# Modulation jobs in batches of four, and own places for the first stage's loads

## The chip, the cores and the metric

One Trainium2 chip; the program runs on one of its cores. The metric is device time in microseconds of one execution. A measurement is several executions, of which the median is given.

## The reference, cut to what matters

Two transformer blocks over 256 latent tokens (and 256 context tokens in the first), width 1024, float32. The first block has two layers; each is a mixer (attention beside a convolution of 31 taps) and a PEER stage (top-k choice among 16384 experts). Each stage is modulated: its input is normed, scaled and shifted by vectors that are products of a conditioning vector with a large matrix.

```python
sc, sc_ctx = silu(c), silu(c_ctx)                 # [1024] each
for l in range(2):
    sh1, s1, g1, sh2, s2, g2 = split(sc @ w_mod[l] + b_mod[l], 6)          # w_mod[l]: 1024 x 6144
    csh1, cs1, cg1, csh2, cs2, cg2 = split(sc_ctx @ w_mod[l] + b_mod[l], 6)
    q, k, v, u = split_cols((rms(x) * (1 + s1) + sh1) @ w_in[l])           # w_in[l]: 1024 x 1792
    ...                                           # attention, convolution, output projection
    x = x + g1 * merge_groups(o_attn, o_conv, ...)
    x = x + g2 * peer(rms(x) * (1 + s2) + sh2, ...)
# second block: nine more vectors from c_2
mod = silu(c_2) @ w_ada + b_ada                   # w_ada: 1024 x 9216
```

## The kernel before, in words

Five engine programs (`sync_program`, `tensor_program`, `scalar_program`, `vector_program`, `gpsimd_program`) run side by side; each engine executes its own in order and they meet at counting semaphores. A `Signal` counts what an engine has finished, a `Book` holds which count a label stands for, so `wait_ge(act, ("mrow", k))` waits until ScalarE has done that piece. Tokens lie along the free axis, channels along the 128 partitions.

**Weights.** SyncE streams 1 MB tiles into a ring of `RING` = 4 slots (`load`, L540 to L549). A load waits until the tile four places back in the order has been read, so one blocked load holds all that stand behind it. `columns` loads one tile of 256 weight columns. Where accuracy asks for it a weight tile is split in a high part (ScalarE, `high`, L1313) and a low part (VectorE, `low`, by `tt` at L1893), and PE multiplies high by high, high by low and low by high.

**Modulation jobs.** The matrices w_mod0, w_mod1 and w_ada are cut in 72 tiles of 256 columns; `JOBS` is their order: four scale tiles of layer 0 (`SCALES`), four shift tiles (`SHIFTS`), the rest of layer 0, layer 1, then w_ada. A job has four steps:
- PE, `mod_rows` (L668): eight products of a 32-column stationary slice of `SC` (three columns hold the silu of c, c_ctx and c_2, the others zero) with the weight tile, in four strips of 32 partitions; the trace shows them as 16 instructions;
- ScalarE, `mods` (L1325): the PSUM bank is copied to `mrow`, two copies of which alternate;
- PE, `mod_sum` (L680): two products with the constant `sel` turn the rows into columns and add the four strips;
- VectorE, `mod_bias` (L1893, for scales L1901): the bias is added and the vector written to `MOD` or `ADA`.

PE does the sum of job k in its `mods` call for job k + 1, ahead of that job's rows, or at once where `flush` is set. Jobs are placed by hand beside other work: 8 in the first stage, `SIDE_JOBS` in the steps of each layer's attention (33 in layer 0, 21 in 18 steps of layer 1), and a few around the modulations. All five programs must count them alike.

**PSUM.** `bank` hands out the eight banks in rotation, skips those in `kept`, and waits for the last reader of the bank. During attention banks 0 to 5 are kept, and jobs, taps and the mean share 6 and 7.

**The first stage** (`mixer(0)` in each program). ScalarE issues the DMAs for `vec` (306 KB of small vectors) and `con` (842.5 KB of constants, L1862), SyncE those for xT and the tiles, in the order: six jobs, the first tile of w_in, two jobs, the other tiles of w_in. ScalarE squares x (L1335), PE sums it with the constant `ones` (L700), ScalarE takes the root (L1342), VectorE inverts (L1951), PE spreads it with `pick` (L716). VectorE multiplies x by scale and root, chunk by chunk of 128 channels (L1901), after each pair the next job's bias. Then it makes the low parts of the first two weight tiles, ScalarE adds the shift and makes the high part of each chunk (L1364), VectorE the low part, and PE multiplies both tiles chunk by chunk (`together`, L730); jobs 6 and 7 are done between the chunks. The other output tiles follow at L651, with the norms of queries and keys (`turning`) between them. The shift of chunks 2j and 2j + 1 comes from shift job j.

**Attention** (`attend`, with `beside` and `side` as the work between its steps). Layer 0 has 32 score tiles, layer 1 sixteen; VectorE works on them in pairs: two maxima (L2014), a scale, a reciprocal, then two calls of `side`, each of 3 or 4 taps of the convolution (7 in layer 1) and a `mods`. PE does scores (L774), a job, the turning of an earlier tile (L656), and every four steps the products with the values (L810). In layer 0 PE also computes six taps of two channel chunks (L651, at steps 0 and 3), which VectorE continues. When all taps are done PE sums the mean at step `MU_AT`. After the steps comes one more `mods`, for which VectorE waits before it takes the mean.

`peer` has three jobs around its modulation.

## Time and profile before

| | us |
|---|---|
| median of three executions | 3174.51 |
| lowest and highest of them | 3168.51, 3174.71 |
| span of the profiled execution, first to last instruction | 3163.5 |
| PE busy in it | 2959.7 (94%) |
| DVE busy | 2440.0 (77%) |
| ACT busy | 1534.7 (49%) |
| POOL busy | 950.4 (30%) |

The profile is of one execution, whose own device time isn't given beside it. PE is TensorE's matmuls, DVE VectorE, ACT ScalarE, POOL GpSimd. Matmul ends are modelled, so a busy PE may be one that waits for nothing but does not run at its peak. Times in the rows count from the first instruction.

### The profile page before, as it was taken

How to read it: one execution, taken by the hardware profiler on the slowest of the kernel's cores; microseconds unless marked ns; L12 is line 12 of the kernel's file. 1: busy time of each engine (PE TensorE's matmuls, PEld its weight loads, DVE VectorE, ACT ScalarE, POOL GpSimd, SP SyncE). 2: the span in 40 equal slices, each digit the busy share in tenths (PEclk: the TensorE clock that was granted, in tenths of full speed). 3: DMA queues.
4: the chain of work that ended last, by engine and by line, in shares of the span. 5: the costliest groups of instructions: out<-in, count | busy, mean ns of one | idle time of the engine just before them, and what ended most of it. 6: DMA issues, size and time to landing. Idle time of an engine off the chain costs nothing.

```text
span 3163.5 us, 48981 instructions
## 1 busy us (share of the span) xinstructions
PE 2959.7 (94%) x19188; PEld 2632.6 (83%) x19188; DVE 2440.0 (77%) x4915; ACT 1534.7 (49%) x2909; POOL 950.4 (30%) x835
## 2 busy tenths in 40 slices
PE   6999999999998999999888999899999899888898
PEld 4656899999998888888766899889999899755898
DVE  3696588898986788888777778897999866578653
ACT  3464346647475333333445466595555542233443
...
GB/s 241 107 345 117 144 173 328 330 255 333 259 329 364 355 360 362 364 374 362 137 179 218 198 268 300 311 350 362 395 400 399 283 238 219 142 34 73 143 137 134
DMA packets 178598, 824.41 MB, mean 261 GB/s; under 512 B 20256, under 2 KB 23872, under 8 KB 138304
## 3 DMA queue, kind: packets, MB, share of 16 engines
...
## 4 chain that ended last, share of the span: by engine, by line
PE 65%; DVE 23%; DMA 6%; ACT 4%; issue 2%; POOL 0%; DVEq 0%; ACTq 0%; POOLq 0%
PE ps L1070 17%; PE ps L989 16%; PE ps L651 12%; DVE fr L1893 5%; DVE area L1901 5%; DMA ring<-in_peer_v 4%; PE ps L1049 4%; DVE area L1893 3%; PE ps L1158 2%; PE ps L730 2%; PE ps L1150 2%; PE ps L918 2%; PE ps L964 1%; DVE acc L1893 1%; ACT fr L1313 1%
## 5 line engine op out<-in xcount | busy, mean ns | idle before, releaser
L1893 DVE TENSOR_TENSOR fr<-ring,fr 128x1024 fp32r<-128x1024 f32 x641 | 782.3, 1223 | 432.2 <-ACT fr L1313 429.3
L1313 ACT CAST fr<-ring 128x1024 fp32r<-128x1024 f32 x677 | 705.2, 1046 | 562.7 <-PE ps L1070 324.5
L989 PE MATMUL ps<-fr 128*128 128x384 f32 (+1 forms) x4784 | 847.4, 330 | 19.5 <-DVE fr L1893 19.4
L989 PEld LDWEIGHTS ps<-fr 128*128 128x128 f32 x4784 | 786.6, 191 | 24.6 <-DVE fr L1893 23.5
L1070 PE MATMUL ps<-fr 128*128 128x512 f32 x2304 | 525.1, 390 | 5.6 <-DVE fr L1893 5.6
L1070 PEld LDWEIGHTS ps<-fr 128*128 128x128 f32 x2304 | 434.4, 189 | 96.2 <-ACT area L1652 5.9
L651 PE MATMUL ps<-fr 128*128 128x256 f32 (+1 forms) x2928 | 408.7, 301 | 4.4 <-DVE fr L1893 4.4
L651 PEld LDWEIGHTS ps<-fr 128*128 128x128 f32 x2928 | 384.9, 191 | 24.9 <-DVE fr L1893 5.2
L2795 POOL DMA_INDIRECT plain<-in_peer_v,area x192 | 289.9, 1510 | 262.0 <-DVE area L1901 169.9
L1095 PE MATMUL ps<-fr 128*128 128x384 f32 x1024 | 297.7, 362 | 12.3 <-DVE fr L1893 11.3
L2827 POOL DMA_DIRECT2D g_scratch<-area x224 | 127.2, 568 | 499.5 <-ACT area L1652 477.1
L1097 PE MATMUL ps<-fr 128*128 128x192 f32 x1024 | 256.4, 250 | 0.0
L1901 DVE SCALAR_TENSOR_TENSOR area<-plain,area 128x1024 f32<-128x1024 f32 x190 | 243.4, 1281 | 1.0
L2788 POOL DMA_INDIRECT plain<-in_peer_u,area x128 | 193.3, 1510 | 123.2 <-DVE plain L2375 103.7
L1652 ACT ACTIVATE area<-ps 128x384 f32<-128x384 f32 (+1 forms) x256 | 106.2, 415 | 216.8 <-PE ps L989 167.2
L1095 PEld LDWEIGHTS ps<-fr 128*128 128x128 f32 x1024 | 192.1, 188 | 20.4 <-DVE fr L1893 19.6
L2810 POOL TENSOR_TENSOR fr<-ring,fr 128x1024 fp32r<-128x1024 f32 x36 | 91.9, 2553 | 362.0 <-ACT fr L1313 361.7
L1097 PEld LDWEIGHTS ps<-fr 128*128 128x128 f32 x1024 | 195.5, 191 | 0.0
L1893 DVE TENSOR_TENSOR area<-area 128x384 f32<-128x384 f32 (+9 forms) x391 | 190.6, 496 | 1.7
L2375 DVE SCALAR_TENSOR_TENSOR plain<-plain,area 128x1024 f32<-128x1024 f32 x128 | 155.6, 1221 | 20.3 <-DMA plain<-in_peer_u,area 20.2
L1615 ACT CAST fr<-area 128x384 fp32r<-128x384 f32 (+1 forms) x256 | 110.2, 430 | 104.7 <-DVE area L1893 104.0
L1049 PE MATMUL ps<-area 128*128 128x128 f32 x1152 | 152.8, 275 | 2.0 <-ACT area L1674 1.5
...
## 6 DMA issues: line engine op xcount, KB each, us to landing
ring<-in_peer_uT SPq DMA_DIRECT2D x128, 1024.0 KB, 6.6
ring<-in_peer_v SPq DMA_DIRECT2D x128, 1024.0 KB, 10.4
...
g_scratch<-area POOLq DMA_DIRECT2D x128, 192.0 KB, 5.7
...
```

The lines of the kernel that those rows point to most:

```text
L651: ins = e.matmul(o, lhs, rhs, start=(n == 0), stop=(n == len(pairs) - 1))
L989: ins = e.matmul(o[:, 0:width], pairs[m][0], pairs[m][1], start=(m == 0), stop=(l == 0 and m == last), skip_group_check=l == 1)
L1049: ins = e.matmul(o[:, 128 * j:128 * j + 128], b.OH[:, half, 0, j, :], b.OH[:, half, 1, j, :], start=True, stop=True)
L1070: ins = e.matmul(M.PS[2 * tb + half][:, :], x[:, r, 128 * tb:128 * tb + 128], v[:, c, 512 * half:512 * half + 512], start=(a == 0 and (r, ...
L1095: e.matmul(M.PS[m][:, b.first:T + D], v[:, 0, 128 * m:128 * m + 128], x[:, :, 0:D], start=(a == 0), stop=False, skip_group_check=True)
L1097: ins = e.matmul(M.PS[m][:, b.first:T], v[:, 1, 128 * m:128 * m + 128], x[:, 0, 0:D], start=False, stop=False, skip_group_check=True)
L1313: e.copy(hi, x).then_inc(act.after(("high", name)), 1)
L1893: return e.tensor_tensor(o, a, b, op).then_inc(dve.after(*labels), 1)
L1901: return e.scalar_tensor_tensor(out=o, in0=a, scalar=s, in1=b, op0=op0, op1=op1).then_inc(dve.after(*labels), 1)
L2375: e.scalar_tensor_tensor(out=x, in0=x, scalar=1.0, in1=b.hx, op0=M_, op1=M_, accum_out=b.dot[:, k:k + 1]).then_inc(dve.after(("urow", l, k ...
L2788: e.indirect_dma_start(b.u_rows[k % U_ROWS], None, A[f"peer_u{l}"], bass.IndirectOffsetOnAxis(ap=b.idx[:, k:k + 1], axis=0)).then_inc(M.u_ ...
L2795: e.indirect_dma_start(b.v_rows[k % n], None, A[f"peer_v{l}"], bass.IndirectOffsetOnAxis(ap=b.idx[:, k:k + 1], axis=0)).then_inc(M.v_row_i ...
```

## The change

- The constants are laid out anew: ones, eps, sel (now 16 columns) and pick first. ScalarE loads those 658 columns; SyncE loads the others later (`rest_in`), and the uses of `blk`, `ident`, `rot`, `cos` and `sin` in layer 0's mixer wait for them.
- The first tile of w_in and the four shift jobs get places of their own in `area` (`EXTRA`), and are issued without a wait behind the four scale jobs.
- `BATCHES`: jobs 0 to 3 are one batch, 4 to 7 single ones, the rest batches of four. The rows of a batch accumulate in one PSUM bank, each job with the stationary slice shifted by four columns so that it fills rows of its own; the bank is `held` over the batch. Eviction, sum and bias are done once per batch, behind its last job. A batch of several jobs takes bank 6 or 7.
- In the first stage all four scales are ready before the first product of x, and the shift jobs' rows are issued right behind; layer 0's attention has 32 side jobs, layer 1's 22.

```diff
@@ -43,14 +43,16 @@
     n = 0
-    for name, w in (("ones", 128), ("blk", 128), ("ident", 128), ("rot", 128), ("cos", 256), ("sin", 256),
-                    ("iota", 128), ("eps", 2), ("sel", 3), ("pick", 512), ("steps", 16)):
+    for name, w in (("ones", 128), ("eps", 2), ("sel", 16), ("pick", 512), ("blk", 128), ("ident", 128), ("rot", 128),
+                    ("cos", 256), ("sin", 256), ("iota", 128), ("steps", 16)):
         CON[name] = (n, w)
...
 _con_layout()
+CON_FIRST = CON["blk"][0]
+EXTRA = (13552, 0, 5872, 7920, 11504)
@@ -60,9 +62,23 @@
                           if kind != "mod0" or m >= 16]
+def _batches():
+    out = [[0, 1, 2, 3], [4], [5], [6], [7]]
+    for k in range(8, len(JOBS)):
+        if (k - 8) % BATCH == 0:
+            out.append([])
+        out[-1].append(k)
+    return out
+BATCH = 4
+BATCHES = _batches()
+PLACE = {k: (g, j) for g, ks in enumerate(BATCHES) for j, k in enumerate(ks)}
 GAP = 2
 LATE_ADA = 48
-SIDE_JOBS = ([1] * 33, [2 if n in (3, 8, 13) else 1 for n in range(18)])
+SIDE_JOBS = ([1] * 32, [2 if n in (3, 7, 11, 15) else 1 for n in range(18)])
 MU_AT = (33, 18)
@@ -293,8 +309,8 @@
         self.ADA = mods[:, 192:264]
-        self.scs = sb("scs", 256)
-        self.SC = self.scs[:, :].rearrange("p (k s) -> p k s", s=32)
+        self.scs = sb("scs", 352)
+        self.SC = self.scs[:, :].rearrange("p (k s) -> p k s", s=44)
         self.mrow = sb("mrow", 512)
@@ -319,8 +335,8 @@
         self.done = {"pe": self.pe, "act": self.act, "dve": self.dve, "pool": self.pool}
-        self.landed = [signal(f"slot{i}_landed", 16) for i in range(RING)]
-        self.vec_in, self.con_in, self.x_in = (signal(f"{e}_in", 16) for e in ("vec", "con", "x"))
+        self.landed = [signal(f"slot{i}_landed", 16) for i in range(RING + len(EXTRA))]
+        self.vec_in, self.con_in, self.rest_in, self.x_in = (signal(f"{e}_in", 16) for e in ("vec", "con", "rest", "x"))
         self.w_stored, self.w_read = ([signal(f"{e}{i}", 16) for i in range(2)] for e in ("w_stored", "w_read"))
@@ -347,14 +363,21 @@
         kind, m = JOBS[k]
+        return self.A["w_ada" if kind == "ada" else f"w_mod{kind[3]}"], 128 * m
+    def batch(self, g):
+        kind, m = JOBS[BATCHES[g][0]]
+        n = 2 * len(BATCHES[g])
         if kind == "ada":
-            return self.A["w_ada"], 128 * m, (2, 1), self.v("b_ada", m, 2), self.ADA[:, m:m + 2]
+            return (2, 3), self.v("b_ada", m, n).unsqueeze(2), self.ADA[:, m:m + n].unsqueeze(2)
         l = int(kind[3])
-        return (self.A[f"w_mod{l}"], 128 * m, (0, 2), self.v(f"b_mod{l}", m, 2).unsqueeze(2).to_broadcast([128, 2, 2]),
-                self.MOD[l][:, m:m + 2, :])
+        return ((0, 2), self.v(f"b_mod{l}", m, n).unsqueeze(2).to_broadcast([128, n, 2]), self.MOD[l][:, m:m + n, :])
...
         s = self.book.slot.get(name, 0)
+        if s >= RING:
+            return self.area[:, EXTRA[s - RING]:EXTRA[s - RING] + n]
         return self.ring[:, s * SLOT:s * SLOT + n]
@@ -557,17 +580,28 @@
             if done[0] < len(JOBS):
-                weights, c0 = M.job(done[0])[:2]
+                weights, c0 = M.job(done[0])
                 columns(("job", done[0]), weights, c0)
                 done[0] += 1
+    def apart(i, name, src):
+        book.slot[name] = RING + i
+        e.dma_start(M.area[:, EXTRA[i]:EXTRA[i] + SLOT], src).then_inc(M.landed[RING + i].after(("here", name)), 16)
...
             if l == 0 and c0 == 0:
-                jobs(6)
+                jobs(len(SCALES))
+                apart(0, ("W", ("in", 0), 0), A["w_in"][0, 0])
+                for i, k in enumerate(range(len(SCALES), len(SCALES + SHIFTS)), 1):
+                    weights, c = M.job(k)
+                    apart(i, ("job", k), weights[c // 256])
+                    done[0] += 1
+                e.dma_start(M.con[:, CON_FIRST:], A["con"][:, CON_FIRST:]).then_inc(M.rest_in.after(("rest",)), 16)
+                continue
             columns(("W", ("in", l), c0), A["w_in"][l], c0)
             if c0 == 0:
-                jobs(GAP if l == 1 else 2)
+                jobs(GAP)
         jobs(sum(SIDE_JOBS[l]))
@@ -626,13 +660,14 @@
     kept = set()
+    held = set()
     own = {}
...
         if among is None:
-            while turn[0] % 8 in kept:
+            while turn[0] % 8 in kept or turn[0] % 8 in held:
                 turn[0] += 1
@@ -659,27 +694,34 @@
     def mod_rows(k):
+        g, j = PLACE[k]
+        last = j == len(BATCHES[g]) - 1
         piece = M.slot(("job", k), 2048).rearrange("p (k m) -> p k m", k=8)
...
         w.wait_ge(act, ("silu",))
-        o = bank(("row", k), (act, ("mrow", k)))
+        o = bank(("row", g), (act, ("mrow", g)), None if last else (6, 7)) if j == 0 else M.PS[book.bank[("row", g)]]
+        if last:
+            held.discard(book.bank[("row", g)])
+        else:
+            held.add(book.bank[("row", g)])
         for i in range(2):
             for q in range(4):
-                ins = e.matmul(o[32 * q:32 * q + 32, 0:256], M.SC[:, 2 * q + i, :], piece[:, 2 * q + i, :], start=(i == 0),
-                               stop=(i == 1))
-        ins.then_inc(pe.after(("row", k)), 1)
-        book.freed.setdefault(("job", k), {})["pe"] = ("row", k)
-    def mod_sum(k):
-        mr = M.mrow[:, 256 * (k % 2):256 * (k % 2) + 256]
+                ins = e.matmul(o[32 * q:32 * q + 32, 0:256], M.SC[:, 2 * q + i, 12 - 4 * j:44 - 4 * j],
+                               piece[:, 2 * q + i, :], start=(j == i == 0), stop=(last and i == 1))
+        ins.then_inc(pe.after(("rows", k), *((("row", g),) if last else ())), 1)
+        book.freed.setdefault(("job", k), {})["pe"] = ("rows", k)
+    def mod_sum(g):
+        mr = M.mrow[:, 256 * (g % 2):256 * (g % 2) + 256]
         w.wait_ge(M.con_in, ("con",))
-        w.wait_ge(act, ("mrow", k))
-        o = bank(("msum", k), (dve, ("mod", k)))
-        c, n = M.job(k)[2]
+        w.wait_ge(act, ("mrow", g))
+        o = bank(("msum", g), (dve, ("mod", g)))
+        n = len(BATCHES[g])
+        o = o[:, 0:8 * n].rearrange("p (j i s) -> p j i s", i=2, s=4)
         for i in range(2):
-            ins = e.matmul(o[:, n * i:n * i + n], mr[:, 128 * i:128 * i + 128], M.c("sel")[:, c:c + n], start=True,
-                           stop=True)
-        ins.then_inc(pe.after(("msum", k)), 1)
+            ins = e.matmul(o[:, :, i, :], mr[:, 128 * i:128 * i + 128],
+                           M.c("sel")[:, 0:4 * n].rearrange("p (j s) -> p j s", s=4), start=True, stop=True)
+        ins.then_inc(pe.after(("msum", g)), 1)
@@ -687,8 +729,10 @@
             if jobs[0] < len(JOBS):
-                mod_rows(jobs[0])
-                jobs[1] = jobs[0]
+                k = jobs[0]
+                mod_rows(k)
+                if k == BATCHES[PLACE[k][0]][-1]:
+                    jobs[1] = PLACE[k][0]
                 jobs[0] += 1
@@ -831,11 +875,9 @@
         if l == 0:
-            mods(1)
+            mods(len(SCALES) - 1)
             roots(("mix", l), b.rstd, 512, ("g", ("mix", l), 7))
-            mods(0, flush=True)
-            for _ in SCALES[1:] + SHIFTS[:2]:
-                mods(1, flush=True)
+            mods(3)
         else:
@@ -850,7 +892,7 @@
         def shifts(k):
-            if l == 0 and 1 <= k <= 4:
+            if l == 0 and k <= 4:
                 mods(k % 2, flush=k % 2 == 0)
@@ -858,6 +900,7 @@
                 return
+            w.wait_ge(M.rest_in, ("rest",))
             n = step[0]
@@ -942,7 +985,7 @@
         roots(("peer", l), b.rstd, T, ("g", ("peer", l), 7))
-        mods(1, flush=l == 1)
+        mods(1, flush=True)
         ready = ("low", "h", ("peer", l), 7)
@@ -1319,11 +1362,14 @@
                 jobs[0] += 1
-                w.wait_ge(pe, ("row", k))
-                if k >= 2:
-                    w.wait_ge(pe, ("msum", k - 2))
-                e.copy(M.mrow[:, 256 * (k % 2):256 * (k % 2) + 256], ps(("row", k))[:, 0:256]).then_inc(
-                    act.after(("mrow", k)), 1)
+                g = PLACE[k][0]
+                if k != BATCHES[g][-1]:
+                    continue
+                w.wait_ge(pe, ("row", g))
+                if g >= 2:
+                    w.wait_ge(pe, ("msum", g - 2))
+                e.copy(M.mrow[:, 256 * (g % 2):256 * (g % 2) + 256], ps(("row", g))[:, 0:256]).then_inc(
+                    act.after(("mrow", g)), 1)
@@ -1450,13 +1496,13 @@
         def shifted(k):
-            if k in (1, 3):
+            if k in (0, 2, 4):
                 mods(1)
-            w.wait_ge(dve, ("mod", len(SCALES) + k // 2))
+            w.wait_ge(dve, ("mod", 1 + k // 2))
...
             modulated(("mix", l), BOTH, 512, shift, b.rstd, HR, lambda k: [("zero",)],
-                      gap=lambda: (mods(len(SCALES) + 2), first()), shifted=shifted)
+                      gap=lambda: (mods(len(SCALES)), first(), mods(1)), shifted=shifted)
         else:
@@ -1542,6 +1588,7 @@
             w.wait_ge(dve, ("turned", l, 4))
+            w.wait_ge(M.rest_in, ("rest",))
             diagonals(0)
@@ -1859,12 +1906,12 @@
     e.dma_start(M.vec[:, :], A["vec"]).then_inc(M.vec_in.after(("vec",)), 16)
-    e.dma_start(M.con[:, :], A["con"]).then_inc(M.con_in.after(("con",)), 16)
+    e.dma_start(M.con[:, 0:CON_FIRST], A["con"][:, 0:CON_FIRST]).then_inc(M.con_in.after(("con",)), 16)
     w.wait_ge(M.vec_in, ("vec",))
     w.wait_ge(dve, ("zero",))
-    e.activation(M.SC[:, :, 0], M.v("c"), ACT.Silu).then_inc(act.after(), 1)
-    e.activation(M.SC[:, :, 1], M.v("c_ctx"), ACT.Silu).then_inc(act.after(), 1)
-    e.activation(M.SC[:, :, 2], M.v("c_2"), ACT.Silu).then_inc(act.after(("silu",)), 1)
+    e.activation(M.SC[:, :, 12], M.v("c"), ACT.Silu).then_inc(act.after(), 1)
+    e.activation(M.SC[:, :, 13], M.v("c_ctx"), ACT.Silu).then_inc(act.after(), 1)
+    e.activation(M.SC[:, :, 14], M.v("c_2"), ACT.Silu).then_inc(act.after(("silu",)), 1)
     e.activation(M.c_own[:, :], M.v("c_2"), ACT.Silu).then_inc(act.after(("c_own",)), 1)
@@ -1926,22 +1973,22 @@
             if jobs[0] < len(JOBS):
-                jobs[1] = jobs[0]
+                g = PLACE[jobs[0]][0]
+                if jobs[0] == BATCHES[g][-1]:
+                    jobs[1] = g
                 jobs[0] += 1
...
-    def mod_bias(k):
-        bias, dst = M.job(k)[3:]
-        o = ps(("msum", k))[:, 0:4].rearrange("p (m s) -> p m s", s=2)
-        if JOBS[k][0] == "ada":
-            o = ps(("msum", k))[:, 0:2]
-        w.wait_ge(pe, ("msum", k))
-        if JOBS[k] in SCALES:
-            stt(dst, o, 1.0, bias, AD, AD, ("mod", k))
+    def mod_bias(g):
+        (s0, s1), bias, dst = M.batch(g)
+        sums = ps(("msum", g))[:, 0:8 * len(BATCHES[g])].rearrange("p (m s) -> p m s", s=4)[:, :, s0:s1]
+        w.wait_ge(pe, ("msum", g))
+        if JOBS[BATCHES[g][0]] in SCALES:
+            stt(dst, sums, 1.0, bias, AD, AD, ("mod", g))
         else:
-            tt(dst, o, bias, AD, ("mod", k))
+            tt(dst, sums, bias, AD, ("mod", g))
@@ -2072,13 +2119,13 @@
         def job(k):
-            if k % 2 == 0:
+            if k == 0:
+                mods(len(SCALES), flush=True)
+                last()
+        def shifted(k):
+            if k in (0, 1, 3, 5):
                 mods(1, flush=True)
-                last()
-        def shifted(k):
-            if k in (0, 3, 5):
-                mods(2 if k == 0 else 1, flush=True)
                 last()
@@ -2105,6 +2152,7 @@
                 w.wait_ge(pe, ("rot", l, i))
+                w.wait_ge(M.rest_in, ("rest",))
                 if i >= 1:
@@ -2348,7 +2396,7 @@
                   lambda k, s: M.MOD[l][:, 24 + k, s:s + 1], b.rstd, HR)
-        mods(GAP, flush=l == 1)
+        mods(GAP, flush=True)
         project(("pq", l), W4, 1024, n_first=2)
@@ -2985,9 +3033,9 @@
     put("eps", np.array([[1e-6, 1e-5]]))
-    sel = np.zeros((128, 3), np.float32)
+    sel = np.zeros((128, 16), np.float32)
     for i in range(4):
-        for j in range(3):
+        for j in range(16):
             sel[32 * i + j, j] = 1.0
...
     pick = np.zeros((128, 512), np.float32)
```

## Rows read from the trace of the kernel before

**Rows 1.** The page: its first line.
```profile
span 3163.5 us, 48981 instructions
```

**Rows 2.** Chain of waits, 0 to 36 us: start us, us, what.
```profile
1.20 12.68 DMA con<-in_con
...
13.93 3.69 PE ps L700 x64
...
27.14 1.67 DVE acc L1901 x4
...
28.94 1.97 PE ps L668 x16
```

**Rows 3.** Timeline, 0 to 110 us: start us, us, engine, line, what, idle before.
```profile
11.31 4.25 ACT L1335 ACTIVATE acc<-xT 128x512 f32<-128x512 f32 x8
...
19.11 1.16 PE L716 MATMUL ps<-area,con 128*128 128x128 f32 x8 [0.19 <-DVE area L1951]
...
20.54 1.07 PE L668 MATMUL ps<-ring,scs 128*32 128x256 f32 x16
...
22.74 0.16 DVE L1901 SCALAR_TENSOR_TENSOR mods<-ps,vec 128x4 f32<-128x4 f32 x1
...
35.97 2.36 DVE L1893 TENSOR_TENSOR fr<-ring,fr 128x1024 fp32r<-128x1024 f32 x2
...
39.18 2.93 PE L730 MATMUL ps<-fr 128*128 128x512 f32 x6 [3.44 <-DVE fr L1901]
...
50.44 1.07 PE L668 MATMUL ps<-ring,scs 128*32 128x256 f32 x16
...
55.66 5.70 PE L730 MATMUL ps<-fr 128*128 128x512 f32 x24
...
61.20 32.80 PE L651 MATMUL ps<-fr 128*128 128x512 f32 x144
```

**Rows 4.** Windows: PE, PEld, DVE, ACT, POOL busy; clock, DMA share, GB/s.
```profile
16.00:20.00 4.00, 3.81 (x56) 2.73 (x49) 0.95 (x1) 0.74 (x2) 0.00 (x0) 1.00 1.02 422
...
28.00:32.00 4.00, 2.58 (x19) 1.32 (x20) 0.79 (x3) 0.37 (x1) 0.00 (x0) 0.58 1.01 365
...
192.00:224.00 32.00, 30.75 (x314) 17.84 (x310) 31.80 (x75) 21.12 (x63) 0.00 (x0) 1.00 0.94 352
...
1684.00:1698.00 14.00, 13.81 (x87) 8.10 (x88) 11.91 (x34) 3.65 (x9) 0.00 (x0) 0.51 0.83 291
```

**Rows 5.** Timeline, the start of layer 0's attention.
```profile
142.93 0.16 DVE L1893 TENSOR_TENSOR mods<-ps,vec 128x4 f32<-128x4 f32 x1 [1.92 <-PE ps L680]
...
149.38 5.42 PE L651 MATMUL ps<-area 128*128 128x512 f32 x12 [0.19 <-DVE mods L1893]
...
157.77 0.75 DVE L1901 SCALAR_TENSOR_TENSOR area<-area,vec 128x512 f32<-128x512 f32 x1 [5.00 <-ACT area L1530]
```

**Rows 6.** Timeline, the end of layer 0's attention.
```profile
235.24 2.07 DVE L1901 SCALAR_TENSOR_TENSOR area<-area,vec 128x512 f32<-128x512 f32 x3
...
242.19 3.60 PE L651 MATMUL ps<-area,con 128*128 128x512 f32 x8
...
249.09 0.16 DVE L1893 TENSOR_TENSOR mods<-ps,vec 128x4 f32<-128x4 f32 x1 [7.91 <-PE ps L680]
```

**Rows 7.** Groups by line, 1624 to 1702 us, DVE: busy, mean ns | idle before.
```profile
L1893 DVE TENSOR_TENSOR mods<-ps,vec 128x2 f32<-128x2 f32 (+1 forms) x21 | 3.2, 154 | 6.1 <-PE ps L680 6.1
```

**Rows 8.** Timeline, the end of layer 1's attention.
```profile
1707.75 0.16 DVE L1893 TENSOR_TENSOR mods<-ps,vec 128x2 f32<-128x2 f32 x1 [6.75 <-PE ps L680]
```

**Rows 9.** Chain of waits, layer 1's second modulation.
```profile
1752.50 1.04 PE ps L668 x16
```

**Rows 10.** DMA issues, 0 to 320 us: KB each, us to landing.
```profile
vec<-in_vec ACTq DMA_DIRECT2D x1, 306.0 KB, 8.6
```

**Rows 11.** Chain of waits, the steady part of layer 0's attention.
```profile
208.81 0.07 DVE mods L1893
```

**Rows 12.** Groups by line, 158 to 224 us, PE.
```profile
L680 PE MATMUL ps<-con,mrow 128*128 128x2 f32 x88 | 13.2, 255 | 1.0 <-DVE mods L1893 0.5 <-ACT mrow L1325 0.4
```

2 lines of the change are left out of this document (1 added, 1 removed).

## The prediction

> **What bounds the kernel now.** I read the page first, for the balance of engines, then the chain of waits, the timeline, the windows and the groups by line in the stages that the diff touches. The page gives a span of 3163.5 us [rows 1]; a gain must come from a stretch in which the modulation jobs or the first loads are on the chain. There are four.
>
> The opening, 0 to 61 us. The chain starts with the constants' transfer (12.68 us); behind it come the sums of squares on PE, to 17.62, then jobs and scale products in turn, and two shift jobs from 28.94 on, the first of which begins only when DVE's last product, at 28.81, has let a PSUM bank go [rows 2]. Then DVE makes the low parts of the first two weight tiles (35.97), PE starts the first projection at 39.18 and reaches the next pair of output tiles at 61.2 [rows 3]. Those 22.0 us hold 48 matmuls that cost 0.24 us apiece where nothing interrupts them (24 in 5.70), so half of the stretch is waiting for jobs 6 and 7 (one of them at 50.44) [rows 3].
>
> Layer 0's attention, 134 to 249 us. In steady state DVE has no gap (31.80 of 32 us), and PE is nearly as full (30.75) [rows 4]. At its start DVE waits 1.92 us for a job's sum and 5.00 us for the second group of taps, which PE begins at 149.38 behind a DVE bias [rows 5]. At its end DVE's last taps stop at 237.3, PE gets to the mean at 242.19, and DVE idles 7.91 us until 249.09 [rows 6].
>
> Layer 1's attention, 1624 to 1708 us. DVE waits 6.1 us for job sums [rows 7] and 6.75 us more at the end [rows 8]; TensorE is granted 0.51 of its clock in the stretch before that end [rows 4].
>
> Layer 1's second modulation, where a job row stands directly on the chain [rows 9]. Layer 0's is alike but smaller.
>
> **The change part by part.**
>
> Constants in two parts. The first part is 658 of 1685 columns. The vector table, ahead of it on ACT's queue, takes 8.6 us to land [rows 10], from 0.76 to 9.4, and the constants land at 13.9 [rows 2]; by share of bytes the first part lands at 9.4 + 0.39 x 4.5 = 11.2, bounds 9.4 and 13.9. ACT's squares run from 11.31 to 15.56 whatever lands [rows 3], and PE's last eight of 64 partial sums take 0.46 us (3.69 / 64 x 8) [rows 2], so the sum of squares ends at 16.0 in place of 17.62. Gain here 1.6, at worst 0. The second part is issued on SP behind nine tiles and first needed after the 61.2 of [rows 3]; at the rate below it is there by 34, so it costs nothing. If it were late, PE's transposes of the values would wait for it.
>
> The scale jobs as one batch. From 16.0, root and reciprocal as now (1.5, from 17.62 to 19.11) stand beside three job rows of 1.07 us, to 19.2; the root's broadcast (1.16) to 20.4; the fourth row to 21.5; eviction and sum, from a row's end at 21.61 to the bias at 22.74, are 1.13, the bias 0.2: 22.8 [rows 3]. Then DVE makes all 16 products with no job between, four times the 1.67 us of four [rows 2]: 29.5, against 28.81 now. So this part by itself loses 2.3, of which the constants give back 1.6. The wait it adds is for the fourth tile ahead of the first product. The DMA engines are full and move 0.37 to 0.42 MB per us [rows 4]; without 0.5 MB of constants among them the fourth tile is complete 1.3 us sooner than now, about 19, under the broadcast.
>
> Shift jobs and the first weight tile without slots. Now the two jobs from 28.94 on hold DVE until 35.97 [rows 2, 3]. After, their tiles are under way from the start (five more issues in SP's first microseconds, with the second constants and the ring's next tiles behind them, none wanted before 50 us), and their rows, evictions and sums fall beside the 6.7 us of products. What is left between the last product and PE's start is one bias 0.16 [rows 6], two low parts of weights 2.36 and one of activations 0.85 (38.33 to 39.18) [rows 3]: 29.5 + 3.4 = 32.9 in place of 39.2. Gain 6.3. The first projection then has 48 matmuls at 0.24 (11.4), two rows and two sums (3.3), and ACT's evictions of jobs 6 and 7, which still stand between its high parts; if PE is at half clock when it starts, as it is now (6 matmuls in 2.93) [rows 3], 2 more. I take 18 us against 22: end at 51 in place of 61.2. **Opening: 10**, bounds 6.3 (the projection as slow as now) and 12.5 (evictions and clock hidden). PE is the bound of the projections behind it, so the shift is kept.
>
> Batches of four in layer 0's attention. The DVE wait of 1.92 at 142.93 goes, as no sum stands there; three rows (3.2), the first of them where the sum is now, and a pair of scores (1.1) put the second taps at 147, 2.4 before 149.38, and with them DVE's resumption at 157.77 [rows 5]. I take 2, bounds 0 and 2.5, because PE's next row meets the bank of the sum just made and waits for DVE's bias. After that each bias costs DVE's stream 0.07 us [rows 11]; 18 of 24 go: 1.3. PE drops three of four sums, 0.75 x 13.2 us over 66 [rows 12], which is slack there. At the end PE is the one behind: between the last tap and the mean's start lie sums, the 33rd job's row (now 32 rows) and a row at half clock [rows 6]. Without them the mean can start just behind the tap, 4.9 sooner; I take 4. **Attention 0: 7.3**, bounds 1 and 9.
>
> Layer 1's attention. The 6.1 us of DVE waits for sums [rows 7] fall from 21 places to six, 15 biases of 0.07 go (1.1), and of the tail of 6.75 [rows 8] a part goes as PE arrives with fewer sums behind it. The last sum still stands after the attention's steps, since job 67 closes a batch in the last one, so the final wait doesn't vanish. I take 6, bounds 1 and 9.
>
> The modulations before the experts. In layer 1 a sum and an eviction go off the chain around the row at 1752.50 [rows 9]: 0.9, the 1.13 of above less what the broadcast hides. In layer 0 0.4; bounds 0 and 2 together. The new flush puts a sum behind an eviction on PE, but PE waits for DVE's first low part there anyway. Stationary slices at an offset, a 16-column sum in place of 2 columns, and a bank held for a batch (seven rotate elsewhere) I cost at nothing: rows and sums keep their instruction counts, and the projections' readers are two tiles behind at most. If that cover fails it is up to 1 us a stage.
>
> Sum: 10 + 7.3 + 6 + 1.3 = 24.6 us off the profiled span of 3163.5. No time is given for that execution itself; the three runs lie at 3168.5 to 3174.7, and I take the sum off their median: 3174.5 - 24.6 = **3150**.
>
> **A rule that speaks against it.** In 28 to 32 us, with PE busy 2.58 of 4 us, the clock was granted 0.58 of 2.4 GHz; it was 1.00 where PE was busy 30.75 of 32 [rows 4], and a job row took 1.97 us at the low level against 1.07 [rows 2, 3]. The Trainium skill's page TensorE: Matmul & The Clock Gate (Part 1) says that the low clock is the default and that steady activity releases it; by that rule, the trace agrees, a PE with fewer sums can lose its clock. Followed to its end this is the third rival.
>
> **The rivals.**
> The opening is bound by its transfers. For: the DMA engines are full to 32 us [rows 4] and nine tiles now stand in one line. Against: at 0.4 MB per us job 7's tile is there by 33, and it is wanted about 43. If late, the opening keeps half, 5: 3155 to 3160. Chance 0.08.
> Only the opening pays: DVE's stream sets both attentions, full as it is [rows 4], and their waits just move. Gain 10 + 1.3 + 2: 3161. Chance 0.13.
> **Slower.** In layer 0's attention PE falls to 1.2 GHz and becomes the bound. Place: the row that opens each batch, which takes the previous sum's bank and waits for DVE's bias, a lump of idle time every four steps. PE's work there becomes 30.75 - 4.8 = 26 of 32 us at full clock, DVE's 31.0; PE decides once over 19% of its work is done at the low level (26 x 1.19 = 31). Wholly low it is 52 against 31, over 66 us plus 43, less 17 from the other stages: 3200. Against: a full PE has its clock [rows 4]. Chance 0.03.
> The change does not reach the chain (jobs 6 and 7, or a bank, give back what is saved; net under 6 us). Chance 0.04.
> The forecast itself 0.72, its own range 3138 to 3160.
>
> **How the numbers follow.** The bounds of the parts sum to gains of 8 and 33. With the runs' own spread of 3 us, and the first two rivals taken in, the range is 3138 to 3163; left out are the last two rivals and the far end of the bounds. About 0.2% (6 us) is what a measurement of this kernel can tell from no change. Faster: 0.72 + 0.13 + 0.08 = 0.93; same 0.04; slower 0.03.
>
> **What would show it.** Right: PE's first partial sum near 11.9 us, 16 products in one run of 6.7 us, the first projection at 33 and its successor near 51; DVE's wait at 142.93 gone; the mean in layer 0's attention within 1 us of the last tap; DVE's waits for sums in layer 1's attention under 3 us. Wrong: PE granted half its clock in the steady part of layer 0's attention, PE waiting for a transfer before 45 us, or layer 1's attention as long as now.

## The result, and the profile after

The changed kernel takes 3149.3 us (median of four executions, 3146.0 to 3150.6) against 3174.6 us for the kernel before (3168.5 to 3179.9, four executions): ratio 0.9928, 95% interval 0.9906 to 0.9949. The sum had said 24.6 us; the two medians are 25.3 apart, and the ratio of the fast runs makes it 22.9. The forecast of 3150 is met. The profiled execution took 3146.0 us with a span of 3144.0, 19.5 less than [rows 1]. The total fits better than its parts: in this profile one term was 5 us too large, two were 3 too small, and stages that nobody edited took 6 back.

The first line of the page after:

```profile
span 3144.0 us, 48460 instructions
```

The opening, the timeline of the changed kernel (start us, us, engine, line, what, idle before). It answers to [rows 3].

```profile
11.68 4.25 ACT L1381 ACTIVATE acc<-xT 128x512 f32<-128x512 f32 x8
...
13.05 3.64 PE L744 MATMUL ps<-acc,con 128*32 128x128 f32 x64 [13.05 <-DMA con<-in_con]
...
23.13 0.17 DVE L1948 SCALAR_TENSOR_TENSOR mods<-ps,vec 128x16 f32<-128x16 f32 x1 [4.96 <-PE ps L722]
23.34 6.35 DVE L1948 SCALAR_TENSOR_TENSOR acc<-xT,mods,ps 128x256 f32<-128x256 f32 x16
...
26.62 1.94 PE L709 MATMUL ps<-area,scs 128*32 128x256 f32 x16 [3.64 <-DMA area<-in_w_mod]
...
34.14 2.93 PE L774 MATMUL ps<-fr 128*128 128x512 f32 x6 [0.70 <-DVE fr L1948]
...
45.66 5.73 PE L774 MATMUL ps<-fr 128*128 128x512 f32 x24 [0.29 <-DVE fr L1948]
...
51.23 11.04 PE L686 MATMUL ps<-fr 128*128 128x512 f32 x48
```

All sixteen products stand in one run, the first projection starts at 34.14 (39.18 before) and the next pair of output tiles at 51.23 (61.20). What now ends last is a tile: PE's row of the first shift job waits 3.64 us for it, and runs at half speed (1.94 us) after that idleness. The chain of waits of the same stretch says the same (start us, us, what):

```profile
4.16 22.42 DMA area<-in_w_mod
26.58 0.04 issue
26.62 1.98 PE ps L709 x16
```

The end of layer 0's attention, timeline, against [rows 6]:

```profile
229.94 3.60 PE L686 MATMUL ps<-area,con 128*128 128x512 f32 x8
...
236.84 0.17 DVE L1940 TENSOR_TENSOR mods<-ps,vec 128x16 f32<-128x16 f32 x1 [7.06 <-PE ps L722]
```

DVE stops at 236.84 - 7.06 = 229.78 (its last tap at 229.71), and PE starts the mean at 229.94, 0.2 us behind the tap and not 4.9. But the last tap itself is only 7.6 us earlier than before, though the stage began 10 us earlier: in between, time was lost. The steady part of the attention shows it. Windows of 64 us (PE, PEld, DVE, ACT, POOL busy; clock, DMA share, GB/s), first before the change, where DVE has no gap and the clock is 1.00, then of the changed kernel:

```profile
158.00:222.00 64.00, 62.95 (x634) 36.76 (x634) 63.62 (x142) 44.56 (x117) 0.00 (x0) 1.00 0.90 341
```

```profile
150.00:214.00 64.00, 56.77 (x560) 28.71 (x558) 60.35 (x121) 38.96 (x100) 0.00 (x0) 0.94 0.91 347
```

and the changed kernel's waits in the same 64 us (us in total, times, longest):

```profile
PE ps L709 <- DVE mods L1940: 7.2, 5, 2.8
...
DVE area L2069 <- ACT area L1459: 3.1, 3, 1.7
```

The first row of a batch (L709) goes into the bank that the last sum has just used, and must wait until DVE has taken that sum with its bias (L1940). DVE does the bias only after its taps. PE then comes late with the turning, ACT with its copy and exponentials (L1459), and at the end of the chain DVE waits for them: the 3.1 us of that wait are nearly all of the 3.3 that DVE is busy less.

Layer 1's attention, the group of DVE's biases, 1614 to 1690 us, against 21 of them in [rows 7]:

```profile
L1940 DVE TENSOR_TENSOR mods<-ps,vec 128x8 f32<-128x8 f32 (+1 forms) x6 | 1.0, 160 | 5.9 <-PE ps L722 5.9
```

and its end in the timeline, against [rows 8]:

```profile
1688.99 0.17 DVE L1940 TENSOR_TENSOR mods<-ps,vec 128x8 f32<-128x8 f32 x1 [5.87 <-PE ps L722]
```

All 5.9 us of the group are this one last wait; inside the attention DVE waits for no sum.

### The profile page after: what moved, and what is told of

It is laid out like the page before. It is cut to its first block, busy times and chain, and to the rows that moved or that the text cites. A ratio compares the mean times of both kernels' runs of the same rounds, so it can differ in the third digit from the quotient of the medians.

```text
span 3144.0 us, 48460 instructions
## 1 busy us (share of the span) xinstructions
PE 2936.0 (93%) x18984; PEld 2608.3 (83%) x18984; DVE 2435.2 (77%) x4864; ACT 1517.0 (48%) x2858; POOL 966.9 (31%) x835
## 4 chain that ended last, share of the span: by engine, by line
PE 65%; DVE 22%; DMA 6%; ACT 4%; issue 2%; POOL 1%; SPq 0%; DVEq 0%; POOLq 0%; ACTq 0%
PE ps L1032 17%; PE ps L1113 17%; PE ps L686 12%; DVE fr L1940 5%; DVE area L1948 5%; PE ps L1092 4%; DVE area L1940 3%; DMA ring<-in_peer_v 2%; PE ps L1201 2%; PE ps L774 2%; PE ps L1193 2%; PE ps L961 2%; PE ps L1007 1%; DVE acc L1940 1%; ACT fr L1356 1%
## 5 line engine op out<-in xcount | busy, mean ns | idle before, releaser
L1940 DVE TENSOR_TENSOR fr<-ring,fr 128x1024 fp32r<-128x1024 f32 (+1 forms) x639 | 780.2, 1223 | 426.0 <-ACT fr L1356 423.6
L1356 ACT CAST fr<-ring 128x1024 fp32r<-128x1024 f32 (+1 forms) x675 | 704.1, 1047 | 552.0 <-PE ps L1113 323.8
L1032 PE MATMUL ps<-fr 128*128 128x384 f32 (+1 forms) x4784 | 854.1, 332 | 22.6 <-DVE fr L1940 22.6
L2843 POOL DMA_INDIRECT plain<-in_peer_v,area x192 | 305.8, 1592 | 252.3 <-DVE area L1948 170.2
L1138 PE MATMUL ps<-fr 128*128 128x384 f32 x1024 | 297.8, 362 | 11.6 <-DVE fr L1940 11.2
L1138 PEld LDWEIGHTS ps<-fr 128*128 128x128 f32 x1024 | 192.2, 188 | 19.1 <-DVE fr L1940 18.3
L1940 DVE TENSOR_TENSOR area<-area 128x384 f32<-128x384 f32 (+9 forms) x391 | 191.0, 497 | 6.2 <-DMA area<-g_scratch 4.5
## 6 DMA issues: line engine op xcount, KB each, us to landing
ring<-in_peer_v SPq DMA_DIRECT2D x128, 1024.0 KB, 10.1
area<-w_scratch POOLq DMA_DIRECT2D x16, 1536.0 KB, 10.4
```

What stands on the lines that cost most here:

```text
L1032: ins = e.matmul(o[:, 0:width], pairs[m][0], pairs[m][1], start=(m == 0), stop=(l == 0 and m == last), skip_group_check=l == 1)
L1138: e.matmul(M.PS[m][:, b.first:T + D], v[:, 0, 128 * m:128 * m + 128], x[:, :, 0:D], start=(a == 0), stop=False, skip_group_check=True)
L1356: e.copy(hi, x).then_inc(act.after(("high", name)), 1)
L1940: return e.tensor_tensor(o, a, b, op).then_inc(dve.after(*labels), 1)
L2843: e.indirect_dma_start(b.v_rows[k % n], None, A[f"peer_v{l}"], bass.IndirectOffsetOnAxis(ap=b.idx[:, k:k + 1], axis=0)).then_inc(M.v_row_i ...
```

## The experiments

A profile is of one execution, so stages are compared by the start of the same matmul in each timeline, less its start in the kernel before (negative is earlier). The marks, by their time before: the end of the opening (61.20 in [rows 3]), the start of layer 0's mean (242.19 in [rows 6]), layer 0's experts' end (1544.1), the first scores of layer 1 (1624.4), its output projection (1712.9), the projection behind its second modulation (1755.1), and the last block (3100.1). Attention 0 is the difference between 134.15 (first scores) and 242.19, attention 1 that between 1624.4 and 1712.9. The times are us; ratio and median are those of the timed executions. The kernel before had a median of 3174.6 beside the change's first one, and of 3166.1 to 3167.3 (11 to 18 executions) in all the later comparisons.

| kernel | 61.2 | attn 0 | 242 | 1544 | 1624 | attn 1 | 1713 | 1755 | 3100 | median | ratio |
|---|---|---|---|---|---|---|---|---|---|---|---|
| the change | -10.0 | -2.3 | -12.3 | -10.5 | -10.2 | -8.9 | -19.1 | -22.5 | -20.3 | 3149.3 | 0.9928 |
| the change again | -9.9 | -1.2 | -11.1 | -9.8 | -6.9 | -6.1 | -13.0 | -16.2 | -13.1 | 3146.7 | 0.9934 |
| batches of one | -10.7 | -1.4 | -12.0 | -12.0 | -8.5 | +4.8 | -3.7 | -6.1 | -3.9 | 3162.9 | 0.9996 |
| one, old places | -9.9 | 0.0 | -10.0 | -9.9 | -9.9 | -1.9 | -11.9 | -14.3 | -10.1 | 3155.8 | 0.9963 |
| batches of two | -10.9 | +9.7 | -1.3 | -2.4 | +0.1 | +5.3 | +5.4 | +3.9 | +8.1 | 3168.3 | 1.0009 |
| two, row bank | -10.5 | -6.7 | -17.2 | -18.5 | -16.0 | -8.2 | -24.2 | -27.0 | -27.6 | 3140.1 | 0.9915 |
| row bank | -11.0 | -7.4 | -18.3 | -15.5 | -15.9 | -7.3 | -23.2 | -25.4 | -23.5 | 3141.7 | 0.9927 |
| row and taps bank | -10.7 | -9.0 | -19.8 | -18.7 | -18.5 | -9.0 | -27.4 | -30.7 | -26.5 | 3139.9 | 0.9910 |
| all four edits | -10.2 | -9.0 | -19.2 | -22.9 | -22.6 | -10.5 | -33.1 | -36.1 | -33.7 | 3134.0 | 0.9891 |
| conflict in layer 1 | -11.1 | -1.7 | -12.9 | -12.4 | -12.1 | -3.9 | -16.0 | -20.8 | -18.4 | 3152.5 | 0.9950 |
| constants whole | -9.4 | -2.0 | -11.5 | -10.6 | -10.4 | -7.2 | -17.5 | -22.3 | -20.1 | 3146.2 | 0.9945 |
| tiles swapped | -7.9 | -0.7 | -8.6 | -7.4 | -4.5 | -6.1 | -10.6 | -13.8 | -13.3 | 3150.2 | 0.9936 |
| shift in ring | -7.3 | -1.2 | -8.5 | -6.9 | -6.6 | -8.9 | -15.5 | -18.8 | -11.6 | 3153.5 | 0.9953 |

**The change once more.** No edit.

> The changed kernel once more, nothing edited: what one profile differs from the next by. If the experts' passes and the last block vary by themselves, single stages of some 100 us differ by 1 to 2 us between the two profiles of this kernel while the attention stages agree within 0.3 us, and the median lies within 3 us of 3149. If instead the 4 us given back in layer 0's expert stage belong to the kernel, they are there again.

Measured: ratio 0.9934 (0.9920 to 0.9949), median 3146.7. The two attentions do not agree within 0.3 us: attention 0 differs by 1.1, attention 1 by 2.8, and the profiled execution (3153.2 us, span 3151.2, 12.3 under [rows 1]) is the slowest of its six. The profiles show where some of it comes from. Ahead of layer 1's scores the same 24 matmuls, first in the changed kernel's first profile, then in the second (timelines):

```profile
1609.82 3.22 PE L686 MATMUL ps<-fr 128*128 128x256 f32 x24
```

```profile
1610.84 5.59 PE L686 MATMUL ps<-fr 128*128 128x256 f32 x24
```

and the windows around them, in the first and in the second:

```profile
1609.00:1615.00 6.00, 4.92 (x32) 4.08 (x34) 3.58 (x10) 0.00 (x0) 0.00 (x0) 1.00 0.07 29
```

```profile
1610.00:1616.00 6.00, 5.82 (x25) 5.64 (x26) 2.64 (x8) 0.00 (x0) 0.00 (x0) 0.50 0.02 10
```

One execution was granted 2.4 GHz there, the other 1.2. So the yardstick for a stage is rough: some 1 us in attention 0 and 3 in attention 1. Runs below that edit something else give more profiles of the same attention code, and they agree: attention 0 is 0.7 to 2.3 us shorter than before in six profiles, attention 1 6.1 to 8.9 in five. The give-back between 318.8 and 1544 is there in both profiles of the change (3.0 and 2.5 us).

**Batches of one.** `BATCH` alone; the opening and the new places of the jobs stay.

```diff
-BATCH = 4
+BATCH = 1
```

> The changed kernel with batches of one job from job 8 on; the four scales stay one batch, so the opening is as changed, and 32 and 22 side jobs stay. Theory (each part adds its own): the opening's 10 us stay and nothing else: second pair of output tiles at 51.2, layer 0's attention from first scores to the mean as long as before (115.0) or 1 shorter, layer 1's as long as before (84); total about 3164, 9 to 11 under before. Rival (the batches give nothing on the chain in layer 0): layer 0's attention no longer than the changed kernel's 112.8. A second rival, that the opening's gain is taken back later in the experts' stages: under 8 in total.

Measured: 3162.9 us, ratio 0.9996 (0.9987 to 1.0006), so not the 9 to 11 us faster that the opening alone should have left. The opening's gain is there at 61.2 and still whole at 1544 (-12.0). Then 3.5 us go ahead of layer 1's scores (the change's two profiles lost 0.3 and 3.0 there), and layer 1's attention takes 4.8 us longer than before, which leaves -3.7. The total alone would have said that the opening was worth nothing. One suspect is the jobs' places: one more stands in layer 1's attention, and the doubled ones in other steps.

**Batches of one in the old places.**

```diff
-SIDE_JOBS = ([1] * 32, [2 if n in (3, 7, 11, 15) else 1 for n in range(18)])
+SIDE_JOBS = ([1] * 33, [2 if n in (3, 8, 13) else 1 for n in range(18)])
```

> Batches of one, and the jobs placed as before the change (33 in layer 0's attention, 21 in layer 1's, with two in steps 3, 8 and 13); all of the opening's changes stay. Theory A (the opening's 10.6 us are kept wherever nothing else changes; batch_of_one lost them because one more job stands in layer 1's attention and three of the doubled ones stand elsewhere, and each stray sum holds DVE there): layer 1's attention takes as long as before the change, the start of its projection pq is 10 to 12 us earlier than before, and the span is 3151 to 3154, ratio near 0.997. Theory B (layer 1's attention meets the opening's shift badly whatever the places are): it is again about 5 us longer than before, span 3158 to 3162, ratio 1.000.

Measured: 3155.8 us, ratio 0.9963 (0.9950 to 0.9976), span 3154.2. Theory A. The opening alone is carried through 1550 us without a change (-9.9, 0.0 in attention 0, -9.9 at 1624), and attention 1 is not longer (-1.9). Against it the batches of one in the new places lose 6.7 us in attention 1 and 3.6 ahead of it: that is what moving the jobs costs while a job still has a sum of its own. Whether it is the places themselves or the banks isn't shown: moving a job also moves the rotation, and in the new places PE's sums wait 12.3 us (8 times) in attention 1 for DVE's bias, 6.5 us (5 times) in the old ones. The opening is worth 10 us, by the profile and by the medians (3166.1 to 3155.8), shown apart from all batching behind the first eight jobs.

**Which bank the first row takes.** The first row of a batch is put into the shared bank that the last sum did not take.

```diff
-        o = bank(("row", g), (act, ("mrow", g)), None if last else (6, 7)) if j == 0 else M.PS[book.bank[("row", g)]]
+        other = (7,) if book.bank.get(("msum", g - 1)) == 6 else (6,)
+        o = bank(("row", g), (act, ("mrow", g)), None if last else other) if j == 0 else M.PS[book.bank[("row", g)]]
```

> The changed kernel, but the rows of a batch take that one of banks 6 and 7 which the sum just made does not have. Theory (the wait of PE's row for DVE's bias, 12.1 us in 7 waits, delays the turned tile, ACT's exponential and so DVE's reciprocal, 1.4 us a batch): PE's waits for DVE's bias fall under 2 us, DVE's four waits of 4.3 us for ACT go, and layer 0's attention from first scores to the mean falls from 112.8 by 3 to 5 us; total 3 to 5 under the changed kernel, about 3145. Rival (DVE's own stream is the bound, PE's wait is slack): within 1 us of the changed kernel. Rival (PE free of the wait runs ahead, idles elsewhere and loses its clock): clock under 0.9 in the steady part and no gain.

Measured: 3141.7 us, ratio 0.9927 (0.9910 to 0.9944). Attention 0 is 7.4 us shorter than before, where the change gave 2.3 and 1.2; neither rival's sign shows. The ratio can't be told from the change's (0.9928 and 0.9934), so it is the stage that carries this reading, and the timed proof comes with the batches of two below. The steady part in the windows:

```profile
150.00:214.00 64.00, 57.52 (x604) 29.45 (x596) 63.62 (x128) 38.86 (x104) 0.00 (x0) 1.00 0.97 377
```

DVE is busy 63.62 of 64 us again, 3.3 more than in the change, with the clock at 1.00; PE's wait for `mods` is gone from the list. Of the 6.1 us that the mean starts earlier than in the change, 3.3 are lost again by 318.8: the mean's own eight matmuls take 5.63 us here and 3.60 in the change, and the first 24 of the output projection 8.40 and 7.11.

**The conflict put into layer 1.** The opposite edit, for layer 1's batches alone: the first row takes the last sum's bank.

```diff
+        same = (book.bank.get(("msum", g - 1)),) if g > 14 else (6, 7)
-        o = bank(("row", g), (act, ("mrow", g)), None if last else (6, 7)) if j == 0 else M.PS[book.bank[("row", g)]]
+        o = bank(("row", g), (act, ("mrow", g)), None if last else same) if j == 0 else M.PS[book.bank[("row", g)]]
```

> The changed kernel, but in layer 1's attention too the rows of a batch take the bank that the sum just made has. Theory (the conflict costs where PE's wait is long enough to reach ACT's exponential): in layer 1 DVE works 5.5 us of taps between two reductions, so PE's wait is up to 3 us a batch in five batches; PE has a third of its time free, so the stage from first scores to the mean grows from 75.6 by 1 to 5 us. Rival (free PE time absorbs it wholly): under 0.5 us. Rival (idle PE loses its clock): PE granted under 0.8 and the stage grows by over 5.

Measured: 3152.5 us, ratio 0.9950 (0.9932 to 0.9968). Attention 1 gains 3.9 us instead of the 6.1 to 8.9 of the five profiles without the edit, and the wait appears in it (waits of PE, 1612 to 1692 us), where neither profile of the change has it:

```profile
PE ps L710 <- DVE mods L1941: 12.2, 4, 7.4
```

So the conflict costs 2 to 5 us there, on the stage's own noise of 3; the interval of the ratio overlaps that of the change, so it is the wait's row that carries this reading. The change itself has no such wait in layer 1 only because of where its rotation happened to stand.

**Batches of two**, without and with that bank choice (`BATCH = 2`; the second kernel also has the row bank's edit).

> Batches of two jobs in place of four, nothing else changed against the changed kernel. Theory A (each sum costs layer 1's attention a wait of DVE, in proportion to the number of sums, 22 with batches of one and 6 with batches of four): layer 1's attention, which gained 15 us between batches of one and of four, gains about 10 of them with 11 sums; span near 3149. Theory B (any batching that lets DVE run through gives all of it): within 2 us of batches of four, span 3143 to 3146. Theory C (the first row of a batch that meets the bank of the last sum is what costs): as many conflicts as sums, and layer 0's attention is 1 to 3 us longer than with batches of four.

> Batches of two, with the first row of a batch put into the shared bank that the last sum did not take. Batches of two alone gave 3168.3, with layer 0's attention 9.65 us longer than before the change (from -10.97 to -1.32 us) and layer 1's 5.3 us longer. Theory A (all of that is the bank conflict, a lump of idle PE each two steps and the clock that it costs): layer 0's attention is 3 to 7 us shorter than before the change, clock 1.00 in its steady part, layer 1's at least 4 us shorter, span 3143 to 3150. Theory B (it is the number of sums and rows): layer 0's attention stays at least 4 us longer than with batches of four and this bank choice, and the span stays above 3155.

Measured: 3168.3 us, ratio 1.0009 (0.9998 to 1.0019), and 3140.1, ratio 0.9915 (0.9899 to 0.9932). These are the clearest two runs of the study: one line between them, and the intervals lie far apart. Batches of two alone make attention 0 longer than before by 9.7 us and attention 1 by 5.3, together more than the opening's whole gain. PE's row waits for DVE's bias 10 times in 64 us of attention 0 (5 times with four) and 9 times in attention 1, where the change has no such wait. That is theory C of the first expectation, at a larger size than it gave. With the other bank both stages gain (6.7 and 8.2 us) and the kernel can't be told from batches of four with the same bank (0.9927, intervals overlapping); theory A of the second expectation. The windows of the steady part, batches of two without and with the edit:

```profile
158.00:222.00 64.00, 53.77 (x494) 28.61 (x498) 55.12 (x113) 34.42 (x92) 0.00 (x0) 0.91 0.86 311
```

```profile
150.00:214.00 64.00, 60.48 (x597) 31.86 (x593) 63.62 (x133) 40.74 (x108) 0.00 (x0) 0.97 0.97 370
```

DVE loses 8.5 of 64 us and gets them all back. The chain of waits of batches of two alone shows one turn of it:

```profile
193.66 0.09 DVE mods L1940
193.74 0.14 issue
193.88 1.94 PE ps L709 x16
195.82 1.05 PE ps L691 x4
196.86 1.09 PE ps L709 x16
197.95 1.88 PE ps L854 x16
```

After this wait of 1.52 us the row runs at half speed (1.94 us), so the idleness costs its length and then some clock. Not each does: behind an equal wait at 181.15 the row took 1.07 us.

**A bank for the taps.** On top of the row bank: PE's taps take the shared bank that the running batch does not hold. In the change the second group (138.02) waited 1.50 us for ScalarE's copy of the rows.

```diff
-                o = bank(("taps", i), (act, ("taps", i)))
+                o = bank(("taps", i), (act, ("taps", i)), (13 - book.bank[("row", PLACE[jobs[0] - 1][0])],))
```

> As row_bank, and the two groups of taps take the bank of 6 and 7 that the open batch does not have. In the changed kernel PE's second taps wait 1.5 us for ACT's eviction of the rows. Theory (that wait is on the chain to DVE's 5.8 us wait for the taps): DVE's first product with the second taps 1.5 us sooner than in row_bank, total 1 to 1.5 us less. Rival: ACT or the diagonals hold it as well, less than 0.5 us.

Measured: 3139.9 us, ratio 0.9910 (0.9891 to 0.9928). The second group of taps starts 1.3 us earlier than with the row bank alone, and the mean 1.4 us earlier, near the 1.5 of the theory. The medians (3139.9 and 3141.7) don't tell the two apart.

**And the ends of the attentions.** On top of both: VectorE takes the mean before it waits for the last sum, and ScalarE makes the high parts of the output weights before the table switch and its job.

```diff
-        mods(1)
         mu = b.tmps[0][:, 0:Tq]
...
             tt(b.y[:, k, 0:Tq], b.y[:, k, 0:Tq], mu, SU, ("mean", l, k))
+        mods(1)
...
-        root_table()
-        mods(1)
         out_high(0, 0)
         out_high(0, 1)
+        root_table()
+        mods(1)
```

> As row_taps_bank, and behind each attention VectorE takes the mean before it waits for the last batch's sum (the mean is there 3 us before that sum in both layers), and ScalarE makes the high parts of the first two output weight tiles before it loads the root's table. Theory (DVE's order puts a sum that nobody needs on the chain): the first output product comes 3 us sooner after the mean's matmuls in each layer, 5 to 6 us in total under row_taps_bank, near 3139. Rival (ACT's parts of the last turned tiles, or PE's own order, hold the start): under 2 us.

Measured: 3134.0 us, ratio 0.9891 (0.9872 to 0.9909), span 3130.6: the fastest version by its median, ahead of both kernels; its interval lies below the change's second one (0.9920 to 0.9949), but overlaps that of the two bank choices alone. Layer 0's output projection, 12.2 us earlier than before in the change, is 22.2 earlier here, and PE waits 1.52 us for DVE's part of it where it waited 4.64 with the bank choices, the 3 us of the theory. Its first 24 matmuls take 5.75 us at full clock (8.51 with the bank choices alone).

```profile
233.35 5.75 PE L962 MATMUL ps<-fr 128*128 128x512 f32 x24 [1.52 <-DVE fr L1941]
```

**The constants in one piece.**

```diff
-    e.dma_start(M.con[:, 0:CON_FIRST], A["con"][:, 0:CON_FIRST]).then_inc(M.con_in.after(("con",)), 16)
+    e.dma_start(M.con[:, :], A["con"]).then_inc(M.con_in.after(("con",)), 16)
...
-                e.dma_start(M.con[:, CON_FIRST:], A["con"][:, CON_FIRST:]).then_inc(M.rest_in.after(("rest",)), 16)
```

> The changed kernel, but all 1698 columns of constants come in one transfer on ACT's queue, as before. Theory (the first part buys 0.9 us: PE's first sum at 13.05 against 13.93, its end at 16.7 against 17.6, but what follows waits for the fourth and fifth tiles of the line): 0 to 1.5 us slower than the changed kernel, the first scale product about 1 us later or less; since 0.5 MB stand among the tiles again, the shift job's row at 26.6 comes 1.3 us later. Rival (the constants set the opening): 1.5 to 3 us slower. Rival (all hidden under the tiles): no difference, PE's rows start later and the second pair of tiles is still at 51.2.

Measured: 3146.2 us, ratio 0.9945 (0.9930 to 0.9959). PE's sums start when the constants have landed, one us later than in the change:

```profile
14.05 3.64 PE L743 MATMUL ps<-acc,con 128*32 128x128 f32 x64 [14.05 <-DMA con<-in_con]
```

The first projection is 0.9 us later and the opening ends 0.5 later than in the change's profiles; the timed runs show no difference. The split is worth a half to one us, not 1.6.

**The order of the tiles, and own places or the ring.** In the first the tile of w_in is issued behind the first two shift tiles instead of ahead of them; in the second these loads go through the ring, in the old order.

```diff
-                apart(0, ("W", ("in", 0), 0), A["w_in"][0, 0])
                 for i, k in enumerate(range(len(SCALES), len(SCALES + SHIFTS)), 1):
+                    if i == 3:
+                        apart(0, ("W", ("in", 0), 0), A["w_in"][0, 0])
```

```diff
-                jobs(len(SCALES))
-                apart(0, ("W", ("in", 0), 0), A["w_in"][0, 0])
...
+                jobs(6)
+                columns(("W", ("in", l), c0), A["w_in"][l], c0)
+                jobs(2)
```

> The changed kernel, but shift tiles 4 and 5 are issued ahead of the first weight tile. In the changed kernel PE waits 3.64 us for tile 4 at 26.62, and the chain begins with its transfer. Theory (the line of tiles is the opening's bound): row 4 at about 24, its bias ready when DVE's products end at 29.7, projection from 34.1 to about 33, total 1 us less. Rival (the weight tile is then late, landing at 29 and made high by 31): no gain or up to 1 us loss.

> The changed kernel, but the first weight tile and the four shift jobs go through the ring in the old order (six jobs, the weight tile, two jobs), behind slots that scale jobs must free. Theory (own places bring jobs 4 to 7 and the weight tile sooner): rows 4 and 5 wait for slots freed at about 17.5 and 18.5, so their tiles land at about 24 and 27, nearly as now; the first weight tile waits for row 2 and lands by 30; jobs 6 and 7 for rows 3 and 4, by 36: the first projection starts at 34 to 36 and ends 1 to 3 us later than 51.2. Rival (own places carry the opening's gain): the projection ends 5 us or more later. Rival (the four scales in one batch ahead of the products and the new placing of the rows carry it all): no difference within 0.5 us.

Measured: 3150.2 us, ratio 0.9936 (0.9917 to 0.9955), and 3153.5, ratio 0.9953 (0.9941 to 0.9966). The opening gains 7.9 and 7.3 us where the change gains 10.0 and 9.9. Swapped, the first shift row needs to wait no more than 0.51 us for its tile, and it helps nothing (timeline):

```profile
23.46 1.07 PE L710 MATMUL ps<-area,scs 128*32 128x256 f32 x16 [0.51 <-DMA area<-in_w_mod]
30.73 1.01 PE L723 MATMUL ps<-con,mrow 128*128 128x4 f32 x4 [6.20 <-ACT mrow L1372]
```

PE waits 6.2 us for the copy of that row, which stands on ScalarE behind the high parts of w_in's tile, and that tile now lands at 28.4 (4.67 + 23.73 in the chain). In the ring it is the same wait (6.19 us). So the own places and the order are worth 2 to 3 of the opening's 10 us. With the half for the constants some 7 are left for the rest of the edit, all scale jobs in one batch ahead of the products and the shift jobs' rows behind them, which no run took apart.

## Why the prediction was right, and where it was not

**The opening, 10 us: right.** Measured 10.0 and 9.9, and alone, with batches of one in the old places, 9.9. Step by step: the first partial sum came at 13.05, not 11.9, as the first constants landed at 13.0 and not by their share of bytes at 11.2; the products started at 23.34 (forecast 22.8) and took 6.35 us (6.7); the projection started at 34.14 (32.9), late because the fifth tile was on the chain until 26.58; the next pair at 51.23 (51). One sign that the text had named for "wrong" did appear, PE waiting for a transfer before 45 us (3.64 us, for the tile of 26.62): the rival of the transfers was right about the place, and wrong in size, as they took 1 us, not 5.

**Attention 0, 7.3 us: wrong, 2.3 and 1.2.** In the first profile the start came to 1.4 (2 forecast). The tail came in full: the mean starts 0.2 us behind the last tap, 4.7 sooner than before (4 forecast). The step that failed is the one between them, "each bias costs DVE's stream 0.07 us [rows 11]; 18 of 24 go: 1.3", with the bank left out: instead of 1.3 gained, some 4 us were lost. The prediction had seen the mechanism, "PE's next row meets the bank of the sum just made and waits for DVE's bias", and priced it at the start alone, at 0.5 of a us; and as the slower rival it tied the loss to PE becoming the bound. PE did not become the bound: the clock went to 0.94, not to half (0.91 in the second profile, with DVE busy 60.41 us against 60.35), and the late turning held DVE through ScalarE. The row bank shows the term: with that wait taken away the stage gains 7.4 us, which is what the prediction had summed for it, the start, the tail and the biases. With batches of two the rival's row, place and sign came true for the stage, which became 9.7 us longer than before, though there too PE was short of its clock (0.91) and not wholly at the low level. The Trainium skill's page TensorE: Matmul & The Clock Gate describes such a case for a bf16 kernel (A second HAM failure mode: psum-queue depth-cycling): a PE that idles briefly between groups as it cycles through banks swings between both clocks, and pays for it between bursts. The trace agrees (0.94 with batches of four and 0.91 with two, against 1.00 with the row bank).

**Attention 1, 6 us: right, 8.9 and 6.1.** DVE's waits for sums inside went from 6.1 us to none. The mechanism holds, the last wait stayed (5.87 us against 6.75) as said. The two profiles are 2.8 us apart, so how much each piece gave can't be said closer than that.

**The modulations, 1.3 us: too small, 4.7 and 4.5.** In layer 1 the change gains 3.4 and 3.2 us between 1713 and 1755. Of this 2.4 are there with batches of one in the old places too, and they are clock, not sums: in the output projection, which lies in that stretch, two groups of 24 matmuls, and eight behind the first, ran slower before: the granted clock around them was 0.50 and 0.67, and is 0.72 and 1.00 (chain of waits, before and then with batches of one in the old places; the change's timeline has 4.64 and 3.14 for them).

```profile
1712.47 5.49 PE ps L918 x24
...
1732.34 4.44 PE ps L918 x24
```

```profile
1700.76 4.63 PE ps L961 x24
...
1719.57 3.14 PE ps L961 x24
```

What is left, some 1 us, is the size that was forecast for the sum and the eviction (0.9). In layer 0 the change gains 1.3 us between 242.19 and 318.8 in both profiles (0.4 forecast), and so does the kernel with the shift tiles in the ring; three other kernels whose code there is the change's (conflict in layer 1, constants whole, tiles swapped) don't (0.1 us gained to 0.3 lost).

**Given back, 6 us, not forecast.** Between 318.8 and 1544 us the gain shrinks by 3.0 us (2.5 in the second profile), and behind 1755 by 3.0, of which 1.6 right behind 2912 (0 there in the second). These stages were not edited. In the experts' stage and at 2912 they come in lumps of 1.5 or 1.6 us; one of them, windows before and after:

```profile
370.00:378.00 8.00, 8.00 (x48) 8.00 (x47) 7.79 (x53) 2.61 (x4) 5.43 (x3) 1.00 0.56 202
```

```profile
356.00:364.00 8.00, 8.00 (x40) 8.00 (x39) 7.79 (x53) 2.27 (x3) 4.31 (x3) 0.82 0.56 205
```

The same stretch, DVE alike to 0.01 us, PE full in both, and 40 matmuls instead of 48: the clock was lower for part of it. The lumps don't come with the change's code as such: of the six profiles with its code in this stage and in layer 0's attention only three have this one, the same three that gain 1.3 us just ahead of it (the change twice and the shift tiles in the ring; they give back 2.5 to 3.0 us by 1544, the others 0.7 to 0.9). The kernels with batches of one, of two, and with the row bank don't have it either. What decides in which execution a lump falls stays open.

In the first profile's sum: 10.0 + 2.3 + 8.9 + 4.7 - 6.4 = 19.5, against 10 + 7.3 + 6 + 1.3 = 24.6. By their ratios the timed runs gave 22.9 and, in the second comparison, 0.9934 of 3166.1, which is 20.9. So by the ratios the saving was 2 to 4 us under the sum. The forecast was met because its misses cancelled, and by luck in the base too: the kernel before read 3174.6 in this comparison and 3166.1 in the one of the second profile, the change 3149.3 and 3146.7. The miss that a reader should look at first is attention 0.
